# One gate unit of the mixer moved from ahead of the first probability transposes to ahead of the second, in TensorE's order

## What is computed

```python
h = rms_norm(x, norm_mix_w[l]) * (1.0 + scale1) + shift1
proj = h @ w_in[l]
hq, hf, hi, hg, sq, sk, sv, gl = jnp.split(proj, split_points, axis=-1)
y_hg = hgrn2_mix(hq, hf, hi, hg, lb_all[l], hg_norm_w[l])
y_sw = swa_sink_mix(sq, sk, sv, q_norm_w[l], k_norm_w[l], sinks[l])
branches = jnp.stack([y_hg, y_sw], axis=2)
y = jnp.einsum('bsnw,nwd->bsnd', branches, w_branch[l])
merge = jax.nn.sigmoid(gl.reshape(B, S, N_BRANCH, D))
mixed = jnp.sum(merge * y, axis=2) @ w_out[l]
```

## Time and profile before

| | us |
|---|---|
| median of three runs | 3588.75 |
| lowest and highest run | 3585.32, 3595.13 |
| span of the profiled execution, first to last instruction | 3586.0 |
| TensorE busy in it | 3358.9 (94%) |
| VectorE busy | 2581.0 (72%) |
| ScalarE busy | 1175.5 (33%) |
| GpSimd busy | 849.9 (24%) |

### The profile page before, as it was taken

The page is one execution under the profiler, slowest core; times in us unless marked ns, Lnnn a source line. Parts: engine busy times, 40 slices in busy tenths (PEclk is TensorE's granted clock), DMA queues, the critical chain, the costliest instruction groups (busy, mean ns, idle before and its releaser), DMA issues. The chain is left out here.

```text
span 3586.0 us, 53735 instructions
## 1 busy us (share of the span) xinstructions
PE 3358.9 (94%) x18867; PEld 3063.5 (85%) x18867; DVE 2581.0 (72%) x4943; ACT 1175.5 (33%) x2011; POOL 849.9 (24%) x904
## 2 busy tenths in 40 slices
PE   5997999899799799999999999998899999999998
PEld 4997999878688799999999999998688888888886
DVE  6435777454688889988988666761777777777777
ACT  3003556442322222237777322222222222222220
POOL 1000111111000011111111566651233333333331
PEclk8998999999899899999999999999999999999999
DMA  6622222154111244546676899984989898989896
GB/s 255 221 99 93 79 90 90 50 185 130 61 47 35 90 145 142 160 145 237 233 268 245 305 342 344 347 314 136 280 284 292 283 294 282 294 281 295 280 294 242
DMA packets 420834, 743.17 MB, mean 207 GB/s; under 512 B 224368, under 2 KB 275744, under 8 KB 416032
## 3 DMA queue, kind: packets, MB, share of 16 engines
q0 software_dynamic: 98624, 369.14, 29.9%
q1 hardware_dynamic: 318624, 318.99, 28.2%
q10 hardware_dynamic: 3392, 52.47, 3.5%
HBM read 607.30 MB, written 133.19 MB: 206 GB/s over the span
## 5 line engine op out<-in xcount | busy, mean ns | idle before, releaser
L466 PE MATMUL apab<-h2hi,auhib 128*128 128x384 f32 x2048 | 706.5, 345 | 43.4 <-DVEq L60 39.0
L467 PE MATMUL apab<-h2lo,auhib 128*128 128x384 f32 x2048 | 688.2, 336 | 0.0
L468 PE MATMUL apab<-h2hi,aulob 128*128 128x384 f32 x2048 | 688.0, 336 | 0.0
L1661 POOL DMA_INDIRECT vrow<-in_expert_v,fw_now x256 | 312.4, 1220 | 716.7 <-DVE acc L1687 699.1
L466 PEld LDWEIGHTS apab<-h2hi,auhib 128*128 128x128 f32 x2048 | 387.7, 189 | 49.1 <-DVEq L60 43.7
L467 PEld LDWEIGHTS apab<-h2lo,auhib 128*128 128x128 f32 x2048 | 387.7, 189 | 0.0
L468 PEld LDWEIGHTS apab<-h2hi,aulob 128*128 128x128 f32 x2048 | 386.9, 189 | 0.0
L1745 ACT ACTIVATE ageb<-apab 128x384 f32<-128x384 f32 x256 | 125.8, 492 | 659.6 <-PE apab L468 640.8
L1687 DVE SCALAR_TENSOR_TENSOR acc<-vrow,fw_share,acc 128x1024 f32<-128x1024 f32 x256 | 327.1, 1278 | 0.9 <-DVE ga L2236 0.5
L2306 PE MATMUL evo<-vhi,Hhi 128*128 128x512 f32 x768 | 300.4, 391 | 12.8 <-DVE acc L2262 8.8
L1710 POOL DMA_DIRECT2D aurb<-in_expert_u x128 | 71.6, 560 | 997.5 <-DVEq L60 697.4
(11 more groups left out here) (319 smaller groups left out, 7412.7 us busy)
## 6 DMA issues: line engine op xcount, KB each, us to landing
aurb<-in_expert_u POOLq DMA_DIRECT2D x128, 512.0 KB, 4.6
vraw<-in_expert_v SPq DMA_DIRECT2D x128, 512.0 KB, 4.0
ahead_dram<-ageb SPq DMA_DIRECT2D x256, 192.0 KB, 4.7
gates_dram<-arena ACTq DMA_DIRECT2D x12, 4096.0 KB, 12.0
ga<-ahead_dram SPq DMA_DIRECT2D x128, 384.0 KB, 5.9
gr<-gates_dram SPq DMA_DIRECT2D x128, 384.0 KB, 7.6
late<-in_w_ada SPq DMA_DIRECT2D x48, 512.0 KB, 5.9
gw<-in_w_in POOLq DMA_DIRECT2D x8, 1408.0 KB, 8.5
```

The costliest lines, as they stand in the source:

```text
L466: pe.matmul(out, lhi, rhi, start=(k == 0), stop=False)
L467: pe.matmul(out, lhi, rlo, start=False, stop=False)
L468: return pe.matmul(out, llo, rhi, start=False, stop=(k == n - 1))
L1661: pool.indirect_dma_start(self.ring[i], None, table, bass.IndirectOffsetOnAxis(ap=self.now[:, h, i:i + 1], axis=0)).then_inc(self.row_in[i ...
```

## The change

The unit `base - 1` stood before `probs(t - 1, 0)` on TensorE; now it stands after level 2 and before `probs(t - 1, 1)`. This holds for the seven tiles t = 1 to 7.

```diff
                     level(t, 1)
                     if t:
-                        gl_unit(base - 1)
                         probs(t - 1, 0)
                     level(t, 2)
                     if t:
+                        gl_unit(base - 1)
                         probs(t - 1, 1)
```

## The result

Slower, where no change was forecast. The changed kernel has a median of 3614.27 us in thirteen runs (3592.45 to 3636.07 in twelve of them) against 3596.12 us in thirteen runs of the kernel before (3585.32 to 3604.17). One run of the changed kernel took 14091.08 us at a mean granted clock of 0.233; the ratio leaves it out, and without it the median is 3613.9 us. The ratio is 1.0054, with a 95% interval of 1.0036 to 1.0073. It lies outside the stated range of 3582 to 3597 us and on the side to which 6% was given. Both kernels spread, the changed one over 44 us; that spread turns out to be part of the answer.

What follows compares the result with a forecast made beforehand. VectorE's unbroken row was taken to set heads_out's start, with TensorE's idle time before it slack; the terms summed to 0, so 3588.5 us, no change (84%), range 3582 to 3597 us.

Steps and rivals of the forecast that it cites:

- What bounds the kernel: Mixer tiles: VectorE sets the pace up to heads_out, TensorE from there on; TensorE's idle time ahead is slack.
- the rows on VectorE say that neither end moves: TensorE's stretch up to the second half's transposes at 418.77: VectorE holds both ends, so the gain is 0.
- ScalarE's slack: ScalarE's copies behind the moved unit: pTc is done 1.06 us before heads_out needs it, so their delay costs nothing.
- The half clock costs 0, and taking it away gives 0: Clock fall before heads_out: transposes to heads_out take 3.44 us at full or half clock, so it is worth 0.
- rival B: After the new hole the clock falls onto the moved unit; heads_out 1.94 us later, 13.6 us in all, 3602 us; 6%.
- The new hole: Between the first half's transposes and level 2, TensorE waits for VectorE's wl, about 1.7 us of issue per tile.
- the Trainium skill's sentence on transposes: Transposes don't count as matmul activity, so 411.68 to 414.26 would be quiet, 2.6 us, and the time rival B's.
- Rival A: The hole before the second half's transposes closes because VectorE's copy comes earlier; saves 15.6 us, 3573 us; 4%.
- C: Time lost at half clock by transposes and a level is given back, 1.7 us in six tiles, 10.3 us, 3578 us; 2%.
- The sum: Whole kernel: 3586.0 + 0 for the profiled execution; the median, 2.75 us above it, stays at 3588.5 us.

Runs made afterwards that it cites:

- changed_vector_first: Changed kernel plus a GpSimd wait: L583 starts only after VectorE's L792 of level 1, so L774 gets in first; 3590.87 us, ratio 0.9982 to before.
- before_vector_first: Kernel before, unit in its old place, plus a GpSimd wait: L583 only after VectorE's L792 of level 1; 3587.22 us, ratio 0.9984 to before.
- before_filled_beside_take: Kernel before, unit in its old place, plus 12 idle matmuls between level 2 and the second half's transposes, beside L792; 3622.13 us, ratio 1.0077.
- gates_behind_decays: before_vector_first with another unit, base+2, and ScalarE's copy of it moved behind decays and the next tile's head; 3596.55 us, ratio 1.0017 to before.
- gates_behind_decays_late_copies: gates_behind_decays with ScalarE's copies of base+3 and base+4 later and eight idle matmuls before heads_out; 3572.81 us, ratio 0.9954 to before.

## Why the prediction was wrong

**What bounds the kernel** was read rightly. VectorE's row from L786 to the second `pTp` copy sets the start of `heads_out`, and TensorE's idle time ahead of it is slack: in changed_vector_first `heads_out` starts at 8.20 us behind L761, before at 8.18, and the holes are 1.39, 0.66 and 1.22 us where 1.6, 0.7 and 1.2 were expected.

**"... the rows on VectorE say that neither end moves"** is the step that failed. In four tiles of seven the row grew by 1.9 us, and `heads_out` started 10.10 us behind L761. I took VectorE's durations as fixed because its list of instructions was unchanged, and asked only which of its instructions wait for TensorE. Two things were on the trace of before and not read. The row's lengths depended on GpSimd's (L786 of 0.90 us where its twin takes 0.43, L851 of 1.63 us where L850 takes 0.69), and L583 followed L774 by 0.01 to 0.03 us in every tile. And TensorE, idle beside L792 before, would be active beside it. A term of 7 us a tile hung on a margin of 20 ns, and it had been put at nothing without looking at GpSimd's timeline at all. My sentence that all of it costs nothing as long as ScalarE's slack holds named the wrong cover.

**"The half clock costs 0, and taking it away gives 0"** was right for a fall ahead of `heads_out`. As a bound it was too narrow: I priced a fall onto the moved unit (rival B) and not onto `heads_out`, the first work behind the slack. A fall there costs 3.2 us, or 5.0 us after a late L774.

**Rival B** came out on the right side and by the wrong way. The new hole of 1.39 us behind the transposes never brought the clock down: the unit ran 0.12 us a matmul in every tile, and its stretch (415.4 to 418.5) was granted 1.00. What the prediction made of the Trainium skill's sentence on transposes ("TensorE: Matmul & The Clock Gate", PE-mode transpose) did not come: eight transposes and the hole behind them, 411.9 to 414.5, were followed by the full clock. Whether a transpose counts as activity is not shown either way by that. Rival A did not come: nothing was gained up to `heads_out`. Nor did C: in changed_vector_first the clock held at 1.00 through the mixer, in before_vector_first it fell in front of `heads_out` (0.96 over the same stretch), and the times are the same. Measured against the kernel before, the loss of 18 us was larger than B's 13.6.

**The sum** as measured in the profile, from L761 to L761 of each tile: four tiles with a late L774, 7.0 to 7.5 us each and 28.7 together, tile 5 with 3.2 us, tile 7 (up to the merge stage) with 2.2, and 0.3 ahead of tile 1. That is the 34.4 us of the mixer, out of 35.4. On the medians it is 18 us: the profiled run of the changed kernel was slower than its median (3623.17 us), and the kernel before seems to have late tiles in some runs. That its runs do is argued from their spread and from its end in before_vector_first; only profiles count tiles, and none of the kernel before has one.

**What is shown and what isn't.** Shown is that TensorE's work beside L792 brings the late L774: put there without the unit it appears, taken away with the unit in place it goes. That the 15 to 20 ns of L792 are the link fits the profiles but wasn't varied by itself. Its length alone doesn't decide a tile: in the three profiled kernels in which TensorE worked beside it and the order was free, L792 took 733 to 749 ns in the eleven late tiles and 731 to 739 ns in the ten others. Which tile is late looks like chance. Why the clock falls within `heads_out` in some tiles with L774 in time (two in the changed kernel, four in before_filled_beside_take, three in gates_behind_decays) and not in others is open.

## What to carry to other kernels

An engine whose instruction list is unchanged can still get slower: before costing a move at nothing, look at the engine next to the bound one too, for pairs of instructions on VectorE and GpSimd that start within a few tens of ns of each other, and settle their order with a wait. Where a program's runs spread by steps, look for such a pair. And after slack ends, ask what the clock of TensorE is at that moment: a hole that costs nothing itself may be paid for at half clock by the work behind it (5.0 us a tile here, which idle matmuls in the holes gave back).

## What the runs showed of the hardware

- At this place VectorE's COPY_PREDICATED from PSUM (128x512) takes 715 to 724 ns with TensorE idle beside it and 729 to 749 ns with matmuls of 256 columns running into another bank (723 to 735 ns beside transposes, in gates_behind_decays_late_copies).
- Which of L774 and L583 gets in first was decided within about 0.02 us, and moved 1.14 us to one engine or 0.54 us to the other (1.83 against 0.69, 1.81 against 1.27).
- `heads_out`, 16 products of 64 columns, takes 3.76 us at the 2.4 GHz level and 7.06 at 1.2 GHz. After a fall within it (tile 5) the clock stayed down for 6.8 us, after one just ahead of it (tile 2) for 13.7 us. In the kernel before, where the fall came ahead of eight transposes and a level, it was 3.4 us.
